# The scores of 32 tokens from gathered rows of expert_u on VectorE instead of TensorE's score passes

## What is computed

```python
def peer_ffn(x, w_pq, sub_keys, expert_u, expert_v):
    q = (xt @ w_pq).reshape(n_tok, PEER_HEADS, 2, PEER_HALF)
    scores = jnp.einsum('thcd,hckd->thck', q, sub_keys)
    s_top, i_top = lax.top_k(scores, PEER_TOPK)
    cand = s_top[:, :, 0, :, None] + s_top[:, :, 1, None, :]
    cand_idx = i_top[:, :, 0, :, None] * PEER_KEYS + i_top[:, :, 1, None, :]
    best, pos = lax.top_k(cand, PEER_TOPK)
    expert_idx = jnp.take_along_axis(cand_idx, pos, axis=-1)
    gate = jax.nn.softmax(best, axis=-1)
    u = jnp.take(expert_u, idx_b, axis=0)
    act = jax.nn.gelu(jnp.einsum('thkd,td->thk', u, xb), approximate=False)
    v = jnp.take(expert_v, idx_b, axis=0)
    return jnp.einsum('thk,thkd->td', g_b * act, v)
```

## Time and profile before

| | |
|---|---|
| median of 3 runs | 1876.7 us (1876.03 to 1881.94) |
| the profiled execution | 1876.2 us |
| its span | 1874.4 us, mean granted clock 0.996 |
| busy: PE, PEld | 99%, 84% |
| busy: DVE, ACT, POOL | 68%, 54%, 56% |
| score stage on PE | 553.8 to 1271.5 us |
| value stage on PE | 1271.5 to about 1862 us |
| DMA | 476 MB, mean 254 GB/s |

### The profile page before, as it was taken

The page is one execution under the profiler, slowest core; times in us unless marked ns, Lnnn a source line. Parts: engine busy times, 40 slices in busy tenths (PEclk is TensorE's granted clock), DMA queues, the critical chain, the costliest instruction groups (busy, mean ns, idle before and its releaser), DMA issues.

```text
span 1874.4 us, 30301 instructions
## 1 busy us (share of the span) xinstructions
PE 1850.5 (99%) x9326; PEld 1572.4 (84%) x9326; DVE 1280.2 (68%) x1886; ACT 1018.8 (54%) x1842; POOL 1055.0 (56%) x769
## 2 busy tenths in 40 slices
PE   9999999999999999999999999999999999999996
PEld 7888888888888888888888888887888888888885
DVE  4555676768565454555555557966898888888887
ACT  4455555545566565555555555555555555555553
POOL 0000231200488989788888887726888666665423
PEclk9999999999999999999999999999999999999998
DMA  7777776664655666788998888977999999999993
GB/s 246 236 240 224 230 239 204 184 204 160 217 170 181 194 186 203 200 192 196 246 230 195 194 192 273 294 232 259 360 390 359 391 338 358 395 375 370 378 341 91
DMA packets 202730, 476.42 MB, mean 254 GB/s; under 512 B 63504, under 2 KB 65744, under 8 KB 201840
## 3 DMA queue, kind: packets, MB, share of 16 engines
q1 hardware_dynamic: 131824, 391.56, 62.0%
q0 software_dynamic: 52416, 80.02, 15.8%
q10 hardware_dynamic: 18432, 4.20, 1.1%
HBM read 453.41 MB, written 21.07 MB: 253 GB/s over the span
## 4 chain that ended last, share of the span: by engine, by line
PE 96%; DVE 2%; DMA 1%; ACT 0%; POOL 0%; issue 0%; SPq 0%; ACTq 0%; DVEq 0%
PE ps L750 25%; PE ps L503 14%; PE ps L505 14%; PE ps L504 14%; PE ps L756 13%; PE ps L790 6%; PE ps L791 6%; PE ps L720 0%; DMA x_nat<-in_x 0%; PE ps L493 0%; DMA act_dram<-halves 0%; DVE stats L1779 0%; PE ps L554 0%; DVE ps L1776 0%; DVE y_out L1801 0%; DVE act_both L1263 0%
## 5 line engine op out<-in xcount | busy, mean ns | idle before, releaser
L750 PE MATMUL ps<-act_both,split_hi 128*128 128x512 f32 x2048 | 513.3, 393 | 0.0
L1059 ACT ACTIVATE split_hi<-raw 128x512 fp32r<-128x512 f32 x512 | 308.0, 625 | 292.2 <-PE ps L756 289.9
L750 PEld LDWEIGHTS ps<-act_both,split_hi 128*128 128x128 f32 x2048 | 368.6, 189 | 65.6
L1509 DVE TENSOR_TENSOR split_lo<-raw,split_hi 128x512 fp32r<-128x512 f32 x368 | 284.0, 788 | 201.7 <-ACT split_hi L1059 197.0
L1179 ACT ACTIVATE v_hi<-v_tile 128x1024 fp32r<-128x1024 f32 x248 | 263.2, 1062 | 254.4 <-PE ps L791 247.0
L1729 DVE TENSOR_TENSOR v_lo<-v_tile,v_hi 128x1024 fp32r<-128x1024 f32 x248 | 308.1, 1265 | 79.1 <-ACT v_hi L1179 78.9
L1250 DVE TENSOR_TENSOR split_lo<-raw,split_hi 128x512 fp32r<-128x512 f32 x304 | 232.5, 771 | 162.1 <-ACT split_hi L846 161.1
L846 ACT ACTIVATE split_hi<-raw 128x512 fp32r<-128x512 f32 x344 | 216.4, 631 | 226.7 <-PE ps L505 224.4
L1927 POOL DMA_INDIRECT gate_dram<-pick_n,places x192 | 300.3, 1564 | 59.4 <-issue 59.4
L1975 POOL DMA_INDIRECT rows<-in_expert_v,picked x128 | 208.4, 1629 | 189.3 <-DVE row_sum L1741 116.7
L756 PEld LDWEIGHTS ps<-act_both,split_lo 128*128 128x128 f32 x2048 | 279.6, 190 | 19.9
(11 more groups left out here) (206 smaller groups left out, 2131.8 us busy)
## 6 DMA issues: line engine op xcount, KB each, us to landing
raw<-in_expert_u SPq DMA_DIRECT2D x256, 512.0 KB
v_tile<-in_expert_v SPq DMA_DIRECT2D x256, 512.0 KB, 7.0
raw<-in_w_in SPq DMA_DIRECT2D x112, 512.0 KB
raw<-in_w_out SPq DMA_DIRECT2D x32, 512.0 KB
raw<-in_w_pq SPq DMA_DIRECT2D x32, 512.0 KB
gate_dram<-zeros SPq DMA_DIRECT2D x24, 512.0 KB, 5.7
gates<-gate_dram POOLq DMA_DIRECT2D x64, 192.0 KB, 4.6
act_dram<-halves ACTq DMA_DIRECT2D x128, 32.0 KB
```

The costliest lines, as they stand in the source:

```text
L750: return nc.tensor.matmul(ps[:, bank, :], split_hi[:, q % SPLITS, i * P:(i + 1) * P], act_both[:, k, :, :].rearrange("p a t -> p (a t)"), ...
L1059: nc.scalar.activation(split_hi[:, q % SPLITS, :], raw[:, q // 2, q % 2, :], ACT.Copy).then_inc(hi_ready, 1)
L1509: vec.tensor_tensor(split_lo[:, q % SPLITS, :], raw[:, q // 2 % RAWS, q % 2, :], split_hi[:, q % SPLITS, :].bitcast(f32), ALU.subtract).th ...
```

## The change

For the last 32 tokens (`OWN`) the scores no longer come from TensorE. Their 32 x 128 picks are laid out as 32 steps of 128 rows (`DOTS`): GpSimd gathers 128 rows of expert_u, 8 KB each, into one of two buffers (`load_u_row`), VectorE multiplies them by the tokens and sums along the row, in two halves of 1024 columns (`dot`), step j during pair 22 + j (`DOT_AT`). VectorE waits for the rows (`u_row_in`) between the low parts of tiles 5 and 6 of the pair. GpSimd's gathers stand in its program between the scatters: two ahead of them, then one behind the scatters number 25, 31, 37 and so on, the last two behind all of them; each of them waits until its buffer was used (`dot_used`). TensorE's passes cover 224 tokens (`UT`): 2 x 224 and 224 columns.

With it come: four loads of the tokens by SyncE (`x1_own`), one more copy in `places_out` and four more small DMAs of GpSimd (`dot_rows`) counted by `picked_in`; the first eight loads of expert_v move to pairs 55 to 62, since they share memory with the row buffers; 32 instead of 48 gate products stand ahead of the value stage; the multiplication of activations and gates moves from GpSimd to VectorE (`weigh`), and `weigh_dots` does it for the 32 tokens after four small DMAs (`move_dots`). `act_dram` holds 32 tokens instead of 64. expert_u is passed twice, in columns and in rows.

```diff
+OWN = HB // 2
+UT = DENSE + OWN
+DOT_SLOTS, DOT_AT = 2, 22
+DOTS = OWN * PKEYS // P
-PREFETCH = 30
+PREFETCH = 55
-APPLIED_AHEAD = 48
+APPLIED_AHEAD = 32
...
+            sp.wait_ge(x1_out, X1_OUT)
+            for g in range(4):
+                sp.dma_start(x1_own[OWN * g:OWN * g + OWN, :], x1_dram[P - OWN:P, PART, :]).then_inc(own_in, 16)
...
-                    return nc.tensor.matmul(ps[:, bank, :], split_hi[:, q % SPLITS, i * P:(i + 1) * P],
-                                            act_both[:, k, :, :].rearrange("p a t -> p (a t)"), start=k == 0,
-                                            stop=k == KT - 1)
+                    return nc.tensor.matmul(ps[:, bank, 0:2 * UT].rearrange("p (a t) -> p a t", a=2),
+                                            split_hi[:, q % SPLITS, i * P:(i + 1) * P], act_both[:, k, :, 0:UT],
+                                            start=k == 0, stop=k == KT - 1)
...
-                    return nc.tensor.matmul(ps[:, bank, 0:SEQ], split_lo[:, q % SPLITS, i * P:(i + 1) * P],
-                                            act_hi[:, k, :], start=False, stop=False)
+                    return nc.tensor.matmul(ps[:, bank, 0:UT], split_lo[:, q % SPLITS, i * P:(i + 1) * P],
+                                            act_hi[:, k, 0:UT], start=False, stop=False)
...
+            act.wait_ge(dot_summed, 1)
+            nc.scalar.activation(dots[:, 0, :], dots[:, 0, :], ACT.Gelu).then_inc(dot_gelu, 1)
...
+            def dot(j, slot, half):
+
+                cols = slice(half * UNIT, half * UNIT + UNIT)
+                part = u_slots[slot][:, cols]
+                vec.scalar_tensor_tensor(out=part, in0=part, scalar=1.0, in1=x1_own[:, cols], op0=ALU.mult, op1=ALU.mult,
+                                         accum_out=dots[:, half, bass.ds(j, 1)]).then_inc(dot_used, 1)
+
-            def u_pair(pair, parity):
+            def u_pair(pair, parity, j=None):
 
                 for k in (2, 3):
                     split_two(pair, parity, k)
+                    if j is not None and k == 2:
+                        dve.wait_ge(u_row_in[parity], pair * 8 - (DOT_AT + parity) * 8 + 16)
+                        dot(j, parity, 0)
                 add_halves(pair, 0, 2 * parity)
                 for k in (4, 5):
                     split_two(pair, parity, k)
+                    if j is not None and k == 4:
+                        dot(j, parity, 1)
...
+            def weigh_dots():
+
+                dve.wait_ge(dot_in, 64)
+                for half in range(2):
+                    some = slice(half * HB + OWN, half * HB + HB)
+                    vec.tensor_tensor(picked_w[some, :], dot_act[some, :], picked_gate[some, :], ALU.mult
+                                      ).then_inc(dot_weighed, 1)
...
+                    def load_u_row(j):
+
+                        if j >= DOT_SLOTS:
+                            pool.wait_ge(dot_used, 2 * (j - DOT_SLOTS) + 2)
+                        eng.indirect_dma_start(u_slots[j % DOT_SLOTS][:, :], None, u_v,
+                                               bass.IndirectOffsetOnAxis(ap=dot_rows[:, j:j + 1], axis=0)
+                                               ).then_inc(u_row_in[j % DOT_SLOTS], 16)
+
+                    def rows_at(h, b, k):
+
+                        n = h * sum(per_head) + b * TOPK + k - h * TOPK
+                        j = DOT_SLOTS + (n - 24) // 6
+                        return j if n >= 24 and n % 6 == 0 and j < DOTS else 0
...
+                            if rows_at(h, b, k):
+                                load_u_row(rows_at(h, b, k))
```

More of the change, by code:

```diff
@@ L1709, in _ @@
             dve.wait_ge(x1_out, X1_OUT)
[L1710 to L1711 removed]
+            dve.wait_ge(picked_in, 128)
+            with dve.Fori(PAIRS_A // 2, DOT_AT // 2) as i:
+                for s in range(2):
+                    u_pair(i * 2 + s, s)
+            dve.wait_ge(own_in, 64)
+            with dve.Fori(DOT_AT // 2, (DOT_AT + DOTS) // 2) as i:
+                for s in range(2):
+                    u_pair(i * 2 + s, s, i * 2 + (s - DOT_AT))
+            dve.wait_ge(dot_used, 2 * DOTS)
+            vec.tensor_tensor(dots[:, 0, :], dots[:, 0, :], dots[:, 1, :], ALU.add).then_inc(dot_summed, 1)
+            with dve.Fori((DOT_AT + DOTS) // 2, PAIRS // 2 - 1) as i:
                 for s in range(2):
@@ L1943, in _ @@
                     pool.wait_ge(zeroed, 16 * ZEROS)
+                    for j in range(DOT_SLOTS):
+                        load_u_row(j)
                     for h in range(PH):
@@ L1950, in _ @@
                             scatter(h, b)
+                    for j in range(DOT_SLOTS + (PH * sum(per_head) - 24) // 6, DOTS):
+                        load_u_row(j)
                     for b in range(TB):
@@ L2069 @@
     arrays, args = {}, []
-    named = [(n, columns_first(np.asarray(inputs[n])) if n == "expert_u" else np.ascontiguousarray(inputs[n]))
-             for n in _INS] + [("tables", cst), ("small_tables", small)]
+    named = [(n, np.ascontiguousarray(inputs[n])) for n in _INS] + [("tables", cst), ("small_tables", small),
+                                                                     ("u_tiles", columns_first(np.asarray(inputs["expert_u"])))]
     for name, a in named:
```

83 lines of the change are left out of this document (58 added, 25 removed).

## The result

The changed kernel takes **1946.6 us** (median of 4 runs, 1935.4 to 1955.3), beside 1876.6 for the kernel before on the same chip: a ratio of 1.036 (95% interval 1.030 to 1.043). The forecast was 1895, in a range up to 1928: the sign was right, the loss is nearly four times as large as forecast. The profiled execution took 1952.1 us (span 1950.0, mean granted clock 0.971 instead of 0.996); every position inside an execution comes from a profiled one, which can lie some us off the median.

A forecast was written before the change was run, and what follows sets the result against it. TensorE bounds the kernel now; after the change GpSimd's scatters and gathers pace much of the score stage. Profiled 1876.2 + 14.1 (score stage) + 4.1 (value stage) = 1894.4; forecast 1895 us, range 1878 to 1928.

The forecast's parts named there:

- TensorE's part: Score stage: narrower passes cut a pair from 11.17 to 9.98 us, giving back 76 us if nothing else were late.
- the narrow pass falls to another price: Rival, score stage: 224-column passes take 0.38 us each instead of getting shorter, total some 2350 us; chance 0.04.
- First loss: Pairs 0 to 17: GpSimd's low halves pace at 10.44 us a pair; pair 18 starts at 743.9 instead of 757.5.
- Second loss: Hand-over to the scatters: an added copy and four small DMAs cost 3.9 us; a late low half costs 4.5 us once.
- Third loss: Paced score stage: six scatters (11.24 us) and a gather (1.65) on GpSimd make 12.89 us a pair for 27 rows.
- The place where a row is waited for: VectorE's wait between low halves in a pair: a row may land 7.0 us after the pair's start without delay.
- The 13 pairs from 51 on: End of score stage: 13 pairs of 9.98 us plus 1.0 us for row 30, 130.7 us; scores end at 1285.6.
- Value stage: Its start: VectorE's gate multiplication waits for scores moved by four small DMAs, delaying TensorE's unit 14 by 4.1 us.
- The rival at 1960: Score stage: the products hold GpSimd as well, 2 x 1.2 us a pair over 27 pairs, +65 us; chance 0.07.
- The other side: Rival, score stage: rows arrive in time if six scatters and a gather take 9.98 us; 1816 us, faster; chance 0.12.
- the clock's fall: TensorE in the score stage: after waits its clock may drop to 1.2 GHz, eating slack, not the path; no term.
- The rule that spoke for worse: GpSimd contends with VectorE's two-SBUF-input instructions, so the new products would slow it, giving 1960 us; scatter rows seemed to contradict.

The follow-up runs named there:

- number 6: Changed kernel with gate products held back until the scores of pair 59 are through, 8 instead of 32 ahead of the value stage: 1937.2 us, ratio 1.032.
- number 2: Changed kernel with each VectorE product covering 32 of its 1024 columns: 1919.9 us, ratio 1.020.
- number 1: Changed kernel with a row gather behind every fourth scatter in place of every sixth: 1893.1 us, ratio 1.006.
- numbers 3 and 4: Changed kernel without row gathers 2 to 31: 1860.3 us, ratio 0.989; the same with products also cut to 32 of 1024 columns: 1844.4 us, ratio 0.980.

## Why the prediction was wrong, step by step

The profiled execution is 1952.1 - 1894.4 = 57.7 us over the sum. By the prediction's own steps:

- **TensorE's part: right.** Half a pair takes 5.05 us (4.99 forecast), the narrow pass 0.88 / 8 = 0.110 us as taken (943.21 to 944.09 above); "the narrow pass falls to another price" did not occur.
- **First loss: wrong, small.** GpSimd does not pace: seven low halves in 8.80 us are 1.26 each, four in 5.03, and the pairs ran at 10.1. In its place stands the 16 us record, 13.24 - 5.05 = 8.2 us in that half pair, 9.1 over the whole pair. Pair 18 starts at 747.8 instead of 743.9.
- **Second loss: right in kind, short.** First gather at 760.0 instead of 755.3, row 2 at 814.3 instead of 805.4: 8.9 us with the step above. About 4 of them are the 25 scatters between, longer already. From the addition that opens the chain to the first gather it took 760.00 - 734.38 = 25.6 us, and the sum has 25.4: that was luck, since the record of 11.6 us stands in it, while the operations behind it and the small DMAs took less than I had taken over.
- **Third loss: the failed step.** "Six scatters are 11.24 us" took the pitch of 1.873 us over from before as if VectorE's new work did not touch it. It is 1.719 + 0.305 = 2.02 us, six are 12.1. The gather I got right (1.404 + 0.31 = 1.71 us against 1.65). The pitch of 13.83 instead of 12.89 is 27 x 0.94 = **25.3 us**. The place where a row is waited for came out 2.7 us better than computed. The reason that I gave, scatter rows that stay at 1540 ns while VectorE is half busy, was one rhythm only: three scatters in step with half a pair, of which one started under the last 0.18 us of a low half. What counts is not how busy VectorE is but what it is doing when a scatter starts. With the new pair, the gathers and the products that step was lost, and 93 of 192 scatters start under a low half or a product.
- **The 13 pairs from 51 on: the second failed term.** 148.6 instead of 130.7 us, 17.9 more: 12.2 are the gate products (number 6), which slow VectorE's low halves to twice their time. I had named these products as work that ends in time and not asked whom they slow; the trace of before already showed 1155 ns. 1.4 are the longer pair, 1.5 row 30, 12.5 us behind row 29 instead of 11.0. The 2.8 left are not assigned.
- **Value stage:** 4.1 us forecast, 12.4 measured, 8.3 more (1952.1 - 1335.0 = 617.1 against 604.7). VectorE waits 5.2 us for the moved scores, which was forecast in kind; the rest is spread: TensorE's waits in this stage are 7.7 us in all instead of 5.3, the clock is 0.97 from 1300 to 1400 us, and what follows its last pass takes 18.6 instead of 13.6 us. Why was not looked at.

8.9 + 25.3 - 2.7 + 17.9 + 8.3 = 57.7. The rival at 1960, GpSimd held by the products, was the closer one: it had 0.07, and its mechanism is shown by numbers 2 to 4, at less than half its price (it had 2.4 us a pair, and the pitch grew by 0.94, of which number 2 gives 0.78 to the products). The other side was a matter of one constant: it decides, as forecast, from a pitch of about 10 us, and with four scatters between rows (number 1) GpSimd reaches it. Of the clock the prediction was right as far as the traces go: passes at 1.2 GHz follow the waits (granted 0.91 of the full clock in 900 to 1000 us), and the pairs still keep GpSimd's pitch, so they ate slack; no run took the clock's fall away by itself.

**The rule that spoke for worse** is now borne out by the runs: the scatters take 1873 ns with products and 1708 without (numbers 3 and 4). The Trainium skill, GPSIMD Engine Reference, Key points, says that GpSimd shares its SBUF interfaces with VectorE and contends with instructions of two SBUF inputs; here the traces agree. The low halves of 1.51 us beside gate products of 1.02 us fit what the Trainium skill, SBUF — State Buffer, Who interferes with whom, says: whichever starts first has the ports and the other waits for its end. The record of 16 us goes further than that page: VectorE was not let in at the ends of twelve instructions of GpSimd and then at that of the thirteenth, and no run here says why.

## What to carry to other kernels

When a step is put behind every n-th instruction of an engine that issues DMAs, count what that engine needs for n of them under the new load, not the old one, and compare it with the consumer's pace; n itself is the cheapest thing to change (six to four gave 53 us). Then follow the gain to the next place where this engine is waited for, and sort its queue by need (another 45 us). Where VectorE and GpSimd both work on SBUF, a duration read from a trace holds for that rhythm alone. Look at the mean beside the median, line up single instructions of the two engines, and see what the other one is doing when each starts; if a few of them take just as long as a period of the other engine (three scatters and half a pair here), the kind value will go with the period.

## What was not expected of the hardware

- VectorE's first instruction after its ranking loop, be it a 128x128 product or a 128x16 copy, was held for 15.8 to 16.0 us in eight of eleven profiled executions of the changed kernel and its edits, while GpSimd ran 128x512 two-operand operations of 1.26 us without a gap, and ended with GpSimd's run in all eight (659.80 and 659.65, 659.87 and 659.84, 661.92 and 661.89). It was absent in the one execution profiled with a wait of 1.76 us on GpSimd, and in two without.
- A 128x256 product of VectorE was held in the same way for 11.54 to 11.64 us in all eleven, up to 0.29 us after GpSimd's last low half; it takes 0.44 us in the kernel before, where GpSimd's low halves come in runs of four.
- VectorE's 128x512 low half takes 0.69 us alone and 1.51 in the median beside GpSimd's 128x384 products.
- A scatter of 128 elements issued by GpSimd has a mean of 1564, 1643, 1708, 1719 or 1873 ns, in kernels that differ in VectorE's products, in the gathers between and in the pace of the pairs. In the changed kernel it takes 1.59 us at most when it starts while no low half and no product runs on VectorE, and ends 1.40 to 1.46 us after that operation's end otherwise (77 of 81 that start over 0.15 us before it). The traces show the times, not the port or lock behind them.
